# A two-layer decoder step: thirteen matmuls at the start, two key products placed earlier, and the fourth half's transpositions placed ahead of the next step's scores

## The chip, the cores and the metric

One NeuronCore of a Trainium2 chip runs the whole program. The metric is the device time of one execution in microseconds (us). TensorE is called PE here, VectorE DVE, ScalarE ACT, GpSimd POOL and SyncE SP; PEld is PE's weight load, which has rows of its own in the profile.

## The reference, cut to what matters

Two decoder layers are applied to 1024 prompt tokens and to 32 sample tokens (8 sequences of 4), which share the weights; the kernel holds them as one block of 1056 columns.

```python
def trunk_layer(x, ...):
    h = rmsnorm(x, nm_pre)
    q_abs, q_pe, c_kv, k_pe, u, v = project(h, pos, w_in, q_norm, w_uq, kv_norm, w_uk, v_norm)
    a_out = attend(q_abs, q_pe, c_kv, k_pe, w_uv)        # latent attention, 8 heads
    g_out = chunk_gating(u, v, w_s, b_s)                 # u * (tril(W_s) v + b), chunks of 128
    x = x + rmsnorm(concat(a_out, g_out) @ w_out, nm_post)
    f = square(relu(rmsnorm(x, nf_pre) @ w_up)) @ w_down
    x = x + rmsnorm(f, nf_post)
```

The prompt attends to its own 1024 keys, causally. Each sample sequence attends to 4096 cached keys besides its own four; they lie in pages of 128 keys that a page table names, so they are gathered page by page.

## The kernel before, in words

Each engine has one program of its own, written out by hand in order, and semaphores join them. Nothing is reordered by a scheduler: what stands ahead on an engine runs ahead. An fp32 product of PE shows as two records each of PE and PEld (two passes).

**Start.** PE waits for the first loads and multiplies the input by the first two column blocks of `w_in` in plain fp32 (L2432, 48 products, 96 records), with the mean of squares between (L2428). Beside it DVE adds up the squares, then makes the low parts `hl` of all eight input blocks (L1684), then takes PE's first accumulators (`take_z`, L1784). The third column block is the first product of split operands (L2479, `dense`). It writes the banks of the first block, so it waits on `acc_free`, which DVE's first `take_z` raises.

**From the projections to the attention.** A loop over nine token blocks (t = 0 to NB, NB = 8) transposes `v` (`turn_v`, L2595), makes one of eight units of q (`q_unit`, L2584) and mixes a chunk (`mix`, L2609). The last `mix` waits for DVE's `bias` of the chunk before (L1863), as both use PSUM bank 7. Behind the loop come eight small products for the sample queries (L2651), a wait for the last q unit, the keys of the first pair of heads (`keys_of`, L2629, two products of 512 columns), the values (`vals_of`, L2616), transpositions of the latent (`turn_c`, L2623 and L2624), the first scores (L2681), more keys and values, and then the steps. ACT and DVE copy each of these out of PSUM. SP first issues the loads of rotated queries and keys, then 16 DMAs of cache pages for step 0 (`gather(0)`, L541). Step 0 needs them at its first `turn_keys` (L2728), and PE waits there on `cache_in`.

**The steps.** Sixteen steps (c = 0 to 15) a layer interleave two things. The prompt's attention has 64 halves: a half i is one head of a job (pair of heads u, query block j), with j in the order 0, 7, 1, 6, 2, 5, 3, 4, and step c takes halves 4c to 4c+3. The paged attention takes 512 cached keys of four sequences a step. A half passes through `scores` on PE (L2681, with the mask in L2684), `maxima` on DVE (L1934), `exps` on ACT (L1189), `normalise` on DVE (L1940, L1943), `turn_p` on PE (L2693, up to 4 transpositions for n = 0 and the rest for n = 1), copies of these out of PSUM (`take_pt`: n = 0 by ACT L1204, n = 1 by DVE L1957), and `values` on PE (L2708, one call for both halves of a job), whose result ACT (L1198) and DVE (L1950) take. The transpositions share two PSUM banks in turn (the ring): each waits until what stands two places ahead has been copied out. The paged part of a step is `turn_keys` (L2728), `step_scores` (L2739, L2741), `step_max` on DVE (L2000), `step_exp` on ACT (L1226, behind `exps(i + 4)` there), `step_turn` (L2749) and `step_values` (L2758); the last two run in the next step. `WIDE_LAST` is true for every step, since the second job of each has j of 4 or more. `following(i)` is `scores(i)` with all its blocks. Each step begins with `values` of the second job of the step before:

```python
                for c in range(STEPS):
                    i, wide_last, first = 4 * c, WIDE_LAST[c], c % CHUNKS == 0
                    if c > 0:
                        values(2 * c - 1)
                        step_turn(c - 1)
```

Of the kernel before, what the change touches and what calls it, by code (L numbers as in the profile page):

```python
# [179 lines left out]
def build(nc, xT, wst, gains, pre, wuq, wuk, wuv, wsp, bsp, cache_c, cache_k, pages, consts,  # L180
          yT, o_cp, o_kp, o_cs, o_ks, o_vs, x_spill):
    with ExitStack() as ctx:
# [1466 lines left out]
        def _(dve):  # L1649
# [38 lines left out]
            for l in range(DEPTH):  # L1688
# [264 lines left out]
                def take_pt(i):  # L1953

                    n = JOBS[i // 2][1] - 3
                    turned(("p", i, 1))
                    dve.tensor_copy(pts[2 * (i % 2) + 1][:, 0:n, :],  # L1957
                                    ring_bank(("p", i, 1))[:, 0:n * P].rearrange(
                                        "p (k n) -> p k n", k=n)).then_inc(t_dve.sem, 1)
# [36 lines left out]
                def step_max(c):  # L1996

                    s = (c % CHUNKS + 1) % 2
                    dve.wait_ge(ds_full.sem, at.value(ds_full, c + c // CHUNKS + 2))
                    dve.tensor_reduce(stat[:, 22:23], ps[7][:, :], AX.X, ALU.max, negate=True)  # L2000
                    dve.drain()
                    dve.tensor_tensor(stat[:, 10 + s:11 + s], stat[:, 22:23], stat[:, 10 + 1 - s:11 + 1 - s],
                                      ALU.min).then_inc(dmax.sem, 1)
# [40 lines left out]
                for c in range(STEPS):  # L2044
                    i, wide_last, first, last = 4 * c, WIDE_LAST[c], c % CHUNKS == 0, c == STEPS - 1
                    if c > 0:
                        take_o(2 * c - 1)
                    if not wide_last:
                        take_pt(i)
                    normalise(i + 1)  # L2050
                    if c > 0:
                        take_ropes(c)
                    maxima(i + 2)
                    if first:
                        new_max(c // CHUNKS)
                    if wide_last:
                        take_keys(c, 2)
                        if c == 0:
                            dve.wait_ge(outs.sem, at.value(outs, 64))
                            take_ropes(c)  # L2060
                        normalise(i + 2)
                    else:
                        take_pt(i + 1)
                        normalise(i + 2)
                        take_keys(c, 2)
                    maxima(i + 3)

                    normalise(i + 3)
                    take_o(2 * c)
                    if c > 0:  # L2070
                        step_out(c - 1)
                    if wide_last:
                        take_pt(i + 2)
                        step_max(c)
                    if not last:
                        maxima(i + 4)
                    if wide_last:
                        take_pt(i + 3)
                    if first:
                        new_out(c // CHUNKS)  # L2080
                    if not wide_last:
                        step_max(c)
                    if not last:
                        normalise(i + 4)
                        maxima(i + 5)
                    if i + 3 in K_AT and K_AT[i + 3][1] == 1:
                        more_keys(K_AT[i + 3][0])
                    step_sum(c)
# [326 lines left out]
        @block.tensor  # L2415
        def _(pe):
            pe.wait_ge(s_init, 2)
            pe.wait_ge(nxt_new.sem, 2)
            for k, units in [(k, (0, 1)) for k in range(KD - 2)] + [(k, (u,)) for u in range(2) for k in (KD - 2, KD - 1)]:
                pe.wait_ge(s_x[k], 16)  # L2420
# [16 lines left out]
            for l in range(DEPTH):  # L2437
# [204 lines left out]
                for t in range(NB + 1):  # L2642
                    if t < NB:
                        turn_v(t + 1)
                    if 0 < t < UNITS_Q:
                        q_unit(t)
                    mix(t)

                pe.wait_ge(vt_free.sem, at.value(vt_free, NB + 1))
# [142 lines left out]
                                     k == first, k == last)  # L2792
                    return ins

                keys_of(0, 0, key_bank(0, 0)[:, :]).then_inc(k_full.sem, 1)
                keys_of(0, 1, key_bank(0, 1)[:, :]).then_inc(k_full.sem, 1)
                for kb in range(4):
                    vals_of(kb)
                pe.wait_ge(mix_free.sem, at.value(mix_free, NB + 1))
# [34 lines left out]
# [5 lines that stand above are left out]
                    for h in range(2):  # L2839
                        turn_p(i + h, 0)  # L2840
                        if h == 1 and not wide_last:
                            turn_p(i + h, 1)
                        scores(i + h + 2, 0)
                        if h == 0 and not wide_last:
                            turn_p(i + h, 1)
                        turn_keys(c, 2 * h)
                        if wide_last:
                            scores(i + h + 2, 1)
                        turn_keys(c, 2 * h + 1)
                        if first and h == 0:  # L2850
                            new_scores(c // CHUNKS)
                        if first and h == 1:
                            new_turn(c // CHUNKS)

                    values(2 * c)
                    if c > 0:
                        step_values(c - 1)
                    if first:
                        new_values(c // CHUNKS)
                    turn_p(i + 2, 0)  # L2860
                    if wide_last:
                        turn_p(i + 2, 1)
                        step_scores(c)
                    following(i + 4)
                    if not wide_last:
                        step_scores(c)
                    turn_p(i + 3, 0)
                    if wide_last:
                        turn_p(i + 3, 1)
                    following(i + 5)  # L2870
                    if i + 3 in K_AT:
                        u, h = K_AT[i + 3]
                        keys_of(u, h, ring(("k", u, h))).then_inc(t_full.sem, 1)
                    if c == STEPS - 1:
                        take_tile()
                        at.step(acc_free)
                        pe.wait_ge(acc_free.sem, at.value(acc_free, -2))
                        pe.wait_ge(exped.sem, at.value(exped, HALVES))
                        pe.wait_ge(gate_l.sem, at.value(gate_l, NB + 1))
                        out_part(0, (4, 5, 6, 7))  # L2880
                        step_turn(c)
                    if c == CHUNKS:
                        pe.wait_ge(on_new.sem, at.value(on_new, 1))
                        pe.transpose(ring(("f", 0))[:, 0:P], oacc[0], ident).then_inc(t_full.sem, 1)
# [374 lines left out]
```

## Time and profile before

| | |
|---|---|
| median of 3 runs | 2466.19 us (2462.88 to 2470.29) |
| the profiled execution | 2470.1 us, span 2468.3 us |
| mean granted PE clock | 0.996 |
| PE busy | 2423.9 us (98%) |
| DVE busy | 1547.9 us (63%) |
| ACT busy | 1021.5 us (41%) |

The time of an execution is a little longer than the span, which reaches from its first instruction to its last. A busy PE is not a PE at its peak, as its records overlap; what counts is the distance between the starts of records. A granted clock of 1.00 is 2.4 GHz and of 0.50 is 1.2 GHz.

### The profile page before, as it was taken

The numbers are of one execution on the slowest core, as the hardware profiler recorded it, in microseconds if no ns is written. First come the engines' busy times: TensorE is split into PE (matmuls) and PEld (weight loads), VectorE is DVE, ScalarE is ACT, GpSimd is POOL, SyncE is SP. The second block draws the span as 40 slices with busy tenths as digits, with TensorE's granted clock in tenths as the row PEclk, the third lists the DMA queues.
The fourth block names the chain that finished last, engine by engine and source line by source line (L and its number), as shares of the span: only waits on it lengthen the run. The fifth ranks groups of instructions, "written<-read, shape, count | busy, mean of one in ns | idle before, by whom it ended". The sixth has DMA issues, their size and how long they took to land.

```text
span 2468.3 us, 49447 instructions
## 1 busy us (share of the span) xinstructions
PE 2423.9 (98%) x19652; PEld 2196.8 (89%) x19652; DVE 1547.9 (63%) x1992; ACT 1021.5 (41%) x1536; POOL 926.8 (38%) x395
## 2 busy tenths in 40 slices
PE   8999999999999999999999999999999999999998
PEld 6996666898999999999979966669889999999998
DVE  5546676349776557755674566662597576557646
ACT  3224666327434333433441255662384333333334
POOL 2432000212664566455213410003046654665441
PEclk9999999999999999999999999999999999999999
DMA  6214333314636544563431143333237356545643
GB/s 218 64 39 112 97 92 85 123 62 147 221 146 219 208 161 150 211 218 138 157 120 46 39 125 92 91 86 114 96 113 296 107 184 225 193 139 181 217 146 152
DMA packets 182355, 347.55 MB, mean 141 GB/s; under 512 B 33968, under 2 KB 46448, under 8 KB 181424
## 3 DMA queue, kind: packets, MB, share of 16 engines
q1 hardware_dynamic: 116128, 207.12, 26.1%
q10 hardware_dynamic: 63504, 129.77, 14.5%
q0 software_dynamic: 2560, 8.39, 1.2%
q8 instruction: 114, 1.87, 0.3%
q14 instruction: 49, 0.40, 0.1%
HBM read 292.94 MB, written 49.06 MB: 139 GB/s over the span
## 4 chain that ended last, share of the span: by engine, by line
PE 89%; DVE 6%; ACT 2%; DVEq 1%; issue 1%; DMA 0%; ACTq 0%; SPq 0%
PE psum L2993 23%; PE psum L3040 21%; PE psum L2479 13%; PE psum L2681 5%; PE psum L2708 3%; PE psum L2464 3%; PE psum L2521 3%; PE psum L2693 3%; PE psum L2728 2%; PE psum L2584 2%; PE psum L2540 2%; PE psum L2432 1%; PE psum L2741 1%; PE psum L2739 1%; PE psum L2758 1%
## 5 line engine op out<-in xcount | busy, mean ns | idle before, releaser
L3040 PE MATMUL psum<-hidh,wh 128*128 128x264 f32 x1312 | 374.1, 285 | 9.6 <-DVE z L2194 5.3
L3040 PE MATMUL psum<-hidl,wh 128*128 128x264 f32 x1312 | 373.6, 285 | 0.0
L3040 PE MATMUL psum<-hidh,wl 128*128 128x264 f32 x1312 | 373.0, 284 | 0.0
L2993 PE MATMUL psum<-hh,wh 128*128 128x264 f32 x1280 | 363.4, 284 | 0.1
L2993 PE MATMUL psum<-hh,wl 128*128 128x264 f32 x1280 | 362.9, 283 | 0.0
L2993 PE MATMUL psum<-hl,wh 128*128 128x264 f32 x1280 | 362.6, 283 | 0.0
L2185 DVE TENSOR_TENSOR z<-psum,z 128x528 f32<-128x528 f32 x336 | 226.1, 701 | 88.2 <-PE psum L3040 88.2
L3040 PEld LDWEIGHTS psum<-hidh,wh 128*128 128x128 f32 x1312 | 246.6, 188 | 11.4 <-issue 8.2
L3040 PEld LDWEIGHTS psum<-hidh,wl 128*128 128x128 f32 x1312 | 247.3, 188 | 0.0
L3040 PEld LDWEIGHTS psum<-hidl,wh 128*128 128x128 f32 x1312 | 247.0, 188 | 0.0
L2993 PEld LDWEIGHTS psum<-hh,wh 128*128 128x128 f32 x1280 | 240.5, 188 | 0.5 <-issue 0.5
L2993 PEld LDWEIGHTS psum<-hh,wl 128*128 128x128 f32 x1280 | 240.6, 188 | 0.0
L2993 PEld LDWEIGHTS psum<-hl,wh 128*128 128x128 f32 x1280 | 240.5, 188 | 0.0
L2479 PE MATMUL psum<-hh,wh 128*128 128x352 f32 x720 | 233.2, 324 | 0.0
L2479 PE MATMUL psum<-hh,wl 128*128 128x352 f32 x720 | 231.1, 321 | 0.0
L2479 PE MATMUL psum<-hl,wh 128*128 128x352 f32 x720 | 230.9, 321 | 0.0
L803 POOL TENSOR_TENSOR wh<-raw,ones 128x1024 fp32r<-128x1024 f32 x36 | 73.4, 2038 | 341.3 <-PE psum L2479 252.2
L819 POOL TENSOR_TENSOR wl<-raw,wh 128x1024 fp32r<-128x1024 f32 x42 | 108.7, 2589 | 187.3 <-ACT wh L1381 184.7
L2175 DVE TENSOR_TENSOR hidl<-z,hidh 128x1056 fp32r<-128x1056 f32 (+1 forms) x100 | 163.6, 1636 | 9.8 <-ACT hidh L1367 9.8
L918 POOL DMA_INDIRECT z<-cache_k,krows x32 | 31.4, 980 | 357.9 <-DVE cn L1970 353.6
L819 POOL TENSOR_TENSOR wl<-sacc,wh 128x1024 fp32r<-128x1024 f32 x38 | 91.5, 2409 | 147.5 <-ACT wh L1381 129.8
L2479 PEld LDWEIGHTS psum<-hh,wh 128*128 128x128 f32 x720 | 135.1, 188 | 1.1 <-issue 0.3
(336 smaller groups left out, 5943.2 us busy)
## 6 DMA issues: line engine op xcount, KB each, us to landing
hh<-h_quarters ACTq DMA_DIRECT2D x60, 1056.0 KB, 5.5
hl<-h_quarters ACTq DMA_DIRECT2D x60, 1056.0 KB, 7.6
raw<-wst SPq DMA_DIRECT2D x48, 512.0 KB, 3.6
z<-cache_c SPq DMA_DIRECT2D x352, 64.0 KB
x<-x_spill SPq DMA_DIRECT2D x4, 4224.0 KB, 14.6
sacc<-wst SPq DMA_DIRECT2D x56, 256.0 KB, 3.2
t<-wst SPq DMA_DIRECT2D x56, 256.0 KB, 3.0
cn<-wst SPq DMA_DIRECT2D x56, 256.0 KB, 4.3
```

What stands on the lines that cost most here:

```text
L803: pool.tensor_tensor(wh[:, s, :], src, ones[:, 0:1].to_broadcast([P, TW]), ALU.mult)
L819: pool.tensor_tensor(wl[:, s, :], src, wh[:, s, :].bitcast(F32), ALU.subtract).then_inc(split.sem, 1)
L2175: dve.tensor_tensor(hid_of(t, hidl)[:, ks, :], src[:, ks, :], hid_of(t, hidh)[:, ks, :].bitcast(F32), ALU.subtract).then_inc(hid_l.sem, 1)
L2185: dve.tensor_tensor(part, dn_banks(u), part, ALU.add).then_inc(dn_free.sem, 1)
L2464: ins = pe.matmul(bank3(u, g), w, m[:, k, cols(g)], start=(first and n == 0), stop=(last and n == 2))
L2479: ins = pe.matmul(bank3(u, g), w[:, s, o:o + P], m[:, k, cols(g)], start=(k == 0 and n == 0), stop=(k == kk - 1 and n == 2))
L2521: ins = pe.matmul(bank, u_w[w], m[:, k, cols(g)], start=(first and n == 0), stop=(last and n == 2))
L2681: ins = pe.matmul(ps[2 * e + h][:, 0:w], qs[e][0:KQ, u, tok(j)], keys[0:KQ, 2 * (u % 2) + e, 512 * h:512 * h + w], start=True, stop=not last)
L2693: ins = pe.transpose(bank[:, (kb % 4) * P:(kb % 4 + 1) * P], probs[e][:, kb * P:(kb + 1) * P], ident)
L2708: ins = pe.matmul(prompt_o[v:v + 32, :], vals[:, kb, 2 * u * VD + v:2 * u * VD + v + 32], pts[2 * e + kb // 4][:, kb % 4, :], start=(kb == ...
L2993: ins = pe.matmul(psum[:, up_bank(st, u) + q, 0:HW], w[:, o:o + P], m[part], start=(fresh and k == 0 and n == 0), stop=(k == 3 and n == 2) ...
L3040: ins = pe.matmul(psum[:, 2 * u + q, 0:HW], w[:, o:o + P], m[:, t, k * HB + q * HW:k * HB + q * HW + HW], start=(fresh and k == 0 and n == ...
```

## The change

Three edits. PE runs 13 products of a 128x128 block of ones with itself, into PSUM bank 7, before it waits for its first load. The first two `keys_of` move from behind the loop over token blocks into its last round, ahead of `mix(8)`; there they wait for seven q units taken by DVE, not for eight. In each step `turn_p(i + 3)` moves ahead of `following(i + 4)` on PE, and on DVE `take_pt(i + 3)` moves ahead of `maxima(i + 4)`.

```diff
@@ vector
+                    if wide_last:
+                        take_pt(i + 3)
                     if not last:
                         maxima(i + 4)
-                    if wide_last:
-                        take_pt(i + 3)
                     if first:
                         new_out(c // CHUNKS)
@@ tensor
             pe.wait_ge(s_init, 2)
+            pe.wait_ge(s_init, 2)
+            for _ in range(13):
+                pe.matmul(ps[7][:, 0:P], ones[:, :], ones[:, :], start=True, stop=True)
             pe.wait_ge(nxt_new.sem, 2)
@@
                     if 0 < t < UNITS_Q:
                         q_unit(t)
+                    if t == NB:
+                        pe.wait_ge(q_dve.sem, at.value(q_dve, UNITS_Q - 1))
+                        keys_of(0, 0, key_bank(0, 0)[:, :]).then_inc(k_full.sem, 1)
+                        keys_of(0, 1, key_bank(0, 1)[:, :]).then_inc(k_full.sem, 1)
                     mix(t)
@@
-                keys_of(0, 0, key_bank(0, 0)[:, :]).then_inc(k_full.sem, 1)
-                keys_of(0, 1, key_bank(0, 1)[:, :]).then_inc(k_full.sem, 1)
                 for kb in range(4):
                     vals_of(kb)
@@
+                    turn_p(i + 3, 0)
+                    if wide_last:
+                        turn_p(i + 3, 1)
                     following(i + 4)
                     if not wide_last:
                         step_scores(c)
-                    turn_p(i + 3, 0)
-                    if wide_last:
-                        turn_p(i + 3, 1)
                     following(i + 5)
```

PE at the end of the loop over token blocks in layer 0, from the mixing of chunk 7 (64x128) on, before. The 64x32 row is `mix(8)`, L2651 the sample queries, and L2629 the keys:

```order
L2609 MATMUL psum<-scratch 64x128 x8
L2609 MATMUL psum<-scratch 64x32 x8
L2651 MATMUL psum<-free_a,cn 128x32
L2651 MATMUL psum<-free_b,cn 128x32
...
L2629 MATMUL psum<-z,sacc 128x512 x2
L2616 MATMUL psum<-rinv,z 128x512 x4
```

The same place in the changed kernel, where `mix` is L2612, the keys L2632, the sample queries L2658 and the values L2619:

```order
L2612 MATMUL psum<-scratch 64x128 x8
L2632 MATMUL psum<-z,sacc 128x512 x2
L2612 MATMUL psum<-scratch 64x32 x8
L2658 MATMUL psum<-free_a,cn 128x32
L2658 MATMUL psum<-free_b,cn 128x32
...
L2619 MATMUL psum<-rinv,z 128x512 x4
```

The two key products moved past `mix(8)` and the eight small products.

PE in step 6 of layer 0, from `step_scores(6)` (L2739, L2741) to `values` of its second job (L2708), before:

```order
L2739 MATMUL psum<-z,sacc 32x512 x4
L2741 MATMUL psum<-cn,sacc 128x512
L2681 MATMUL psum<-scratch,free_a 128x512
L2684 MATMUL psum<-trir,idr 128x128
L2693 MATMUL psum<-cst,z 128x128 x6
L2681 MATMUL psum<-scratch,free_b 128x512
L2684 MATMUL psum<-trir,idr 128x128
L2708 MATMUL psum<-t,scratch 32x128 x24
```

The same place in the changed kernel, where L2746 and L2748 are `step_scores`, L2700 is `turn_p`, L2688 and L2691 are `scores`, and L2715 is `values`:

```order
L2746 MATMUL psum<-z,sacc 32x512 x4
L2748 MATMUL psum<-cn,sacc 128x512
L2700 MATMUL psum<-cst,z 128x128 x6
L2688 MATMUL psum<-scratch,free_a 128x512
L2691 MATMUL psum<-trir,idr 128x128
L2688 MATMUL psum<-scratch,free_b 128x512
L2691 MATMUL psum<-trir,idr 128x128
L2715 MATMUL psum<-t,scratch 32x128 x24
```

The six transpositions moved ahead of the first of the two score blocks, so that both score blocks now stand between them and `values`.

DVE in step 0 of layer 0, from `step_max` (L2000, L2002) on, as a difference; L1957 is `take_pt(3)` and L1934 is `maxima(4)`:

```order
 L2000 TENSOR_REDUCE stat<-psum 128x1
 L2002 TENSOR_TENSOR stat<-stat 128x1
-L1934 TENSOR_REDUCE stat<-psum 128x1
-L1957 COPY t<-psum 128x512
+L1957 COPY t<-psum 128x512
+L1934 TENSOR_REDUCE stat<-psum 128x1
 L1991 COPY stat<-stat 128x1
 L1993 COPY z<-psum 128x128
```

The copy and the reduction have changed places. The orders of ACT, POOL and SP are the same in both kernels.

## Rows read from the trace of the kernel before

**Rows 1.** Page: the chain that ended last, by engine

```profile
PE 89%; DVE 6%; ACT 2%; DVEq 1%; issue 1%; DMA 0%; ACTq 0%; SPq 0%
```

**Rows 2.** Windows: stretch, length, busy by engine, granted clock, DMA share, GB/s

```profile
201.50:208.30 6.80, 6.80 (x18) 4.15 (x18) 4.65 (x14) 3.29 (x6) 2.36 (x3) 0.50 0.53 117
1423.50:1430.30 6.80, 6.80 (x15) 3.80 (x15) 4.35 (x14) 2.98 (x6) 2.76 (x3) 0.50 0.58 129
608.50:611.00 2.50, 0.95 (x8) 0.76 (x8) 2.41 (x3) 1.19 (x3) 0.00 (x0) 1.00 0.67 210
```

**Rows 3.** Timeline of the start, PE and PEld: start, us, instruction, count

```profile
7.98 20.85 PE L2432 MATMUL psum<-x,z 128*128 128x352 f32 x60 [7.98 <-DMA x<-xT]
...
13.39 0.34 PEld L2432 LDWEIGHTS psum<-x,z 128*128 128x128 f32 x1 [0.25 <-issue]
...
13.88 14.39 PEld L2432 LDWEIGHTS psum<-x,z 128*128 128x128 f32 x49
...
41.12 0.19 PEld L2479 LDWEIGHTS psum<-hh,wh 128*128 128x128 f32 x1
```

**Rows 4.** Timeline of the start, DVE

```profile
23.59 15.53 DVE L1684 SCALAR_TENSOR_TENSOR hl<-x,gpre,hh 128x1056 fp32r<-128x1056 f32 x8
...
39.11 1.25 DVE L1784 TENSOR_TENSOR z<-psum,rinv 128x1056 f32<-128x1056 f32 x1
```

**Rows 5.** Timeline of PE ahead of the steps, layer 0

```profile
198.24 1.09 PE L2609 MATMUL psum<-scratch 128*64 128x128 f32 x16
200.22 0.65 PE L2609 MATMUL psum<-scratch 32*64 32x32 f32 x16 [0.89 <-DVE scratch L1863]
...
203.74 3.78 PE L2629 MATMUL psum<-z,sacc 128*128 128x512 f32 x4
...
222.00 0.60 PE L2728 MATMUL psum<-cst,z 128*128 128x128 f32 x4
```

**Rows 6.** DMA ahead of the steps: SP's queue, then windows of both layers

```profile
208.00 10.05 SPq L541 DMA_DIRECT2D z<-cache_c  x16
...
219.20:222.00 2.80, 2.74 (x11) 1.23 (x10) 1.71 (x6) 1.82 (x6) 0.00 (x0) 1.00 0.00 0
1440.00:1443.60 3.60, 3.60 (x13) 1.61 (x12) 2.61 (x7) 2.72 (x10) 0.00 (x0) 1.00 0.00 0
```

**Rows 7.** Timeline of PE, layer 1: its first `turn_keys`

```profile
1443.64 0.60 PE L2728 MATMUL psum<-cst,z 128*128 128x128 f32 x4
```

**Rows 8.** Lines of PE in the steps of layer 0: busy, mean ns, idle before, releasers

```profile
L2708 PE MATMUL psum<-t,scratch 128*32 128x128 f32 x1152 | 38.1, 275 | 4.2 <-ACT t L1204 1.8 <-DVE z L1993 1.0 <-DVE t L1957 0.9
```

**Rows 9.** Timeline of PE and ACT, end of step 3, layer 0

```profile
276.84 0.60 ACT L1204 ACTIVATE t<-psum 128x512 f32<-128x512 f32 x1 [2.31 <-PE psum L2693]
...
277.78 1.30 PE L2708 MATMUL psum<-t,scratch 128*32 128x128 f32 x40 [0.58 <-ACT t L1204]
```

**Rows 10.** Timeline of PE, end of step 12, layer 0

```profile
406.51 0.60 PE L2681 MATMUL psum<-scratch,free_a 96*128 96x256 f32 x2
...
409.45 1.96 PE L2708 MATMUL psum<-t,scratch 128*32 128x128 f32 x64 [0.91 <-DVE t L1957]
```

**Rows 11.** Timeline of DVE, end of step 12, layer 0

```profile
406.63 0.69 DVE L1957 COPY t<-psum 128x512 f32<-128x512 f32 x1
...
408.07 0.42 DVE L1934 TENSOR_REDUCE stat<-psum 128x1 f32<-128x256 f32 x1
408.41 0.68 DVE L1957 COPY t<-psum 128x512 f32<-128x512 f32 x1
```

**Rows 12.** Timeline of PE, DVE and ACT, end of step 6, layer 0

```profile
320.37 0.82 PE L2693 MATMUL psum<-cst,z 128*128 128x128 f32 x6
...
320.57 0.69 DVE L1934 TENSOR_REDUCE stat<-psum 128x1 f32<-128x512 f32 x1
...
322.17 0.69 ACT L1226 ACTIVATE z<-psum,stat 128x512 f32<-128x512 f32 x1
...
323.56 0.66 PE L2749 MATMUL psum<-cst,z 128*128 128x128 f32 x4
```

## The prediction

> **What bounds the kernel now.** I read the page first. PE sets the end: 89% of the chain that ended last is PE, 6% DVE [rows 1]. So an edit pays only where PE starts something earlier that it does not then wait for. Next I asked the windows for the granted clock, since a span can be full of PE records and still be slow: it is 1.00 nearly everywhere, but 0.50 from 201.5 to 208.3 us in layer 0 and from 1423.5 to 1430.3 in layer 1 [rows 2]. Those are the stretches between the projections and the attention. The first matmuls are slow too, which the clock column does not tell (no clock record lies ahead of them). The loads do: at 13.39 one takes 0.34 us behind 0.25 idle, 0.59 a record, and from 13.88 on 49 take 14.39 us, 0.294 a record [rows 3]. So PE began at 1.2 GHz at 7.98 and came to 2.4 GHz near 13.8 us. Last I read the timelines around the three edits, to see who would hold PE if PE were earlier, and the groups by line inside the steps, where `values` (L2708) has 4.2 us of idle time ahead of it per layer [rows 8]; the same stretch of layer 1 gives the same row.
>
> **Edit 1, the thirteen products at the start.** They are 26 records of 128 columns. The nearest fp32 row, 6 transpositions of 128 columns in 0.82 us [rows 12], is about 0.14 a record, so 0.28 at the lower clock: 7.3 us at most. PE now waits until 7.98 for its input [rows 3], so they lie in that wait, save for some tenths if PE is slow to start them. If the clock has risen by 7.98, the 60 records up to L2428 take 60 x 0.294 = 17.6 us instead of 20.7, and PE is 3.1 us earlier. Who holds it then? The first split product (L2479, loads at 41.12 [rows 3]) writes banks that DVE's L1784 must free, and that ends at 39.11 + 1.25 = 40.36. Ahead of it DVE has the eight L1684, 15.53 us from 23.59 without a gap to L1784 [rows 4]: DVE never waits for PE there, so it will not move. PE can start at about 40.36 + 0.13 = 40.5, not at 38.0. The gain is 41.12 - 40.5 = **0.6 us**, and PE gets a new pause of about 2.4 us.
>
> The Trainium skill (TensorE: Matmul & The Clock Gate, Part 1) says that the throttled state is the default and activity releases it, and its Terms put the penalty at the throttled time times (1 - K/N). By that the warm-up would be worth half of the 5.8 us of slow records, 2.9 us, and the sum below 12.4 instead of 10.1. The rows agree on the two levels, but not on what this is worth here, as DVE sets the date.
>
> **Edit 2, the keys.** Before, mixing chunk 7 is over near 199.3, PE is idle 0.89 us until 200.22 (it waits for DVE's L1863), and the keys start at 203.74, at the lower clock: 4 records in 3.78 us [rows 5], about half of that at 2.4 GHz. Afterwards they run from 199.3 to 201.0. `mix(8)` starts 0.8 us later than now. Behind it DVE does not suffer: its L1863 for that block comes long after. So 1.7 us of work goes into a pause of 0.9 plus a delay of 0.8 that is earned back where the keys stood: 0.9 us gained. The second part is the clock. It fell at 201.5, 1.3 us behind that pause and the small products on both sides of it. With 1.7 us of dense work in the pause I take it to stay at 1.00. A stretch with only 0.95 us of PE in 2.50 kept 1.00 elsewhere [rows 2]. The work of 6.8 us then takes 3.4: 3.4 us gained. PE would come to the first `turn_keys` 4.3 us earlier, at 222.00 - 4.3 = 217.7 in layer 0 and 1443.64 - 4.3 = 1439.3 in layer 1 [rows 5, 7].
>
> There stands what is late next: the gather of step 0. SP issues its 16 DMAs from 208.00 for 10.05 us, behind loads whose dates DVE and POOL set, and none of that moves. DMA is busy until about 219.2 and silent from there on, in layer 1 until 1440.0 [rows 6]. So PE goes on at about 219.35 and 1440.1: 222.00 - 219.35 = **2.65 us** in layer 0, 1443.64 - 1440.1 = **3.5 us** in layer 1. Everything behind is issued in order from there. Of the 8.6 us that PE gains, 2.4 are lost to the gather.
>
> **Edit 3, the steps.** PE is nearly gapless in them; idle time stands ahead of `values` alone, 4.2 us a layer [rows 8]. It waits there for the copies of the transpositions, which now have only one score block as cover; with two, the copies come earlier. That bounds the gain at 8.4 us. But DVE holds it. Step 12: DVE ends `step_max` at 408.07, does `maxima` (0.34 to the next start), then the copy at 408.41, and `values` starts 1.04 later at 409.45 [rows 10, 11]. With the two exchanged, the copy starts at 408.07, if its transpositions are there. They would start at 406.51, but the last four wait for the bank that DVE empties by 407.3, and are done near 408.0. `values` then starts at 409.11: 0.34 gained of 0.91. Step 0 has the same widths and gives about the same. In step 3 the last copy is behind ACT's 276.84 + 0.60 [rows 9]. Afterwards DVE's copy, behind `step_max` at 277.0, ends at about 277.3 and `values` starts near 277.6: 0.15 of 0.58; steps 7 and 11 are alike. Steps 1 and 13 I put at 0.25 each. With 512 columns in the score block (step 6) there is no idle time to win. Per layer 2 x 0.35 + 3 x 0.15 + 2 x 0.25 = 1.65, **3.3 us** for both, and the ends are 0 and 8.4; I take the lower part, since I can name DVE's date in each.
>
> What is pushed back: the first score block, by up to 0.65 us in step 6. `maxima` follows at about 321.2 instead of 320.57, and ACT's two exponentials follow it. `step_turn` at 323.56 waits for L1226, now over at 322.9 [rows 12]: 0.7 of slack for 0.5 of delay. That cover costs nothing, but it is thin.
>
> **Sum.** 0.6 + 2.65 + 3.5 + 3.3 = 10.1 us. The profiled execution, 2470.1 (span 2468.3 and 1.8 around it), becomes 2460.0. It was 3.9 above the median of the runs, so against 2466.19 the sum gives **2456.1 us**.
>
> **The rivals.**
> - *The clock falls in a pause that the change makes.* PE gets pauses of 2.4 us ahead of L2479 and of 1.6 and 0.7 us ahead of `turn_keys`; before 201.5 it fell at a pause of 0.89 with light work beside. For: the new pause at the start is longer than the 1.55 us in the window at 608.5, which is the longest that kept 1.00. Against: dense products stand on both sides. One fall as long as the old ones costs up to 3.4 us of PE (6.8 x 0.5), half that if it is half as long; the sum is then 7 to 8 and the time about 2459. If the old fall also stays in both layers, only about 2 x 0.9 is left of edit 2, the sum is near 6 and the time 2460. The skill's same page (Part 1, HAM oscillation and the psum-queue failure mode) holds that short idle times between groups throw the clock back; by that this rival would be the rule. In the steps it is not borne out: 0.9 us pauses at their ends left the clock at 1.00. I give it 27%.
> - *The start pays in full*, because DVE's L1684 are short if POOL's work beside them falls otherwise. Then 3.1 instead of 0.6: 2453.6. DVE's rows have no gap to close, so 4%.
> - *The new order holds PE in the steps.* The score block comes 0.65 us later, DVE puts 0.34 to 0.6 of copy ahead of `maxima`, and the chain `maxima`, `exps`, `step_exp`, `step_turn` has 0.7 of slack. If both delays add (0.65 + 0.42 = 1.07), each of some 30 steps loses 0.35, 10.5 us, and the 3.3 are gone as well: sum -3.7, about 2470. Against it: DVE does the copy in the time in which it would wait for the later scores. It decides from 1.0 us of delay on, as 0.3 a step uses up the other gains. 5%.
> - *The gain ahead of the steps is lost further on*, for instance as loads for rotated keys or the copies of ACT and DVE hold PE before `turn_keys`: edit 2 gives 2 us, the sum 6, 2460. 9%.
> - My forecast: 55%.
>
> **How the numbers follow.** A measurement of this kernel can tell about 0.3% (7.4 us) from no change. The forecast and the full start lie beyond that bound, with scatter (the runs before spread over 7.4 us) most of their 59% but not all; of the first and fourth rival about half does. That gives 0.72 faster, 0.23 the same and 0.05 slower. The range goes down by the part of 8.4 and of 3.1 that I left out, to 2449, and up to the sum of 4 or so of the weaker cases, 2463.
>
> **What the profile after would show.** Edit 1: loads of 0.19 from 7.98 on; L1784 still near 39.1; the first split product near 40.5 behind DVE. Edit 2: keys from about 199 less 0.6; a granted clock of 1.00 up to the steps; PE idle ahead of the first `turn_keys`, released by DMA. Edit 3: L2708's idle time down from 4.2 to about 2.5 a layer, and none new ahead of L2749 or L2693. The prediction is wrong if the clock column shows 0.50 again, if L1684 moved, if the gather moved, or if L2749 has waits.

## The result, and the profile after

The changed kernel takes 2469.99 us (median of 22 runs, 2467.43 to 2471.47), the kernel before 2466.60 (22 runs, 2462.59 to 2471.53). The ratio is 1.0013, with a 95% interval of 1.0007 to 1.0019. So the change costs about 3 us: less than the 0.3% that the prediction called measurable in one comparison, and outside its range of 2449 to 2463.

The page and the granted clock of the changed kernel first. The chain answers to [rows 1]: PE went from 89% to 84% of it, so more of the chain is something that PE waits for.

```profile
span 2468.8 us, 49500 instructions
...
PE 84%; DVE 8%; ACT 2%; issue 2%; DVEq 2%; DMA 1%; SPq 0%; ACTq 0%; POOL 0%; POOLq 0%
```

Then the windows of the changed kernel (stretch, length, PE busy with its records, granted clock, DMA share, GB/s), beside [rows 2]:

```profile
41.00:44.40 3.40, 3.40 (x14) 0.50 0.45 171
...
204.80:208.20 3.40, 3.40 (x5) 0.51 0.77 175
...
1426.90:1430.20 3.30, 3.30 (x5) 0.50 0.91 200
```

Ahead of the last microseconds of the program the clock falls three times instead of twice. The old falls start 3.4 us later, end at the same dates as before and so last half as long, and a new one stands at 41.0 us. What is ahead of that one shows in the timeline of the start (start, length, instruction, count, idle time ahead of it), beside [rows 3, 4]:

```profile
1.14 5.88 PE L2420 MATMUL psum<-ones 128*128 128x128 f32 x26 [1.14 <-POOL eps L790]
7.49 1.42 PE L2435 MATMUL psum<-x,z 128*128 128x352 f32 x4 [0.47 <-DMA x<-xT]
...
38.97 2.41 DVE L1784 TENSOR_TENSOR z<-psum,rinv 128x1056 f32<-128x1056 f32 x2
...
40.47 0.40 PE L2482 MATMUL psum<-hh,wh 128*128 128x352 f32 x1 [2.25 <-DVE z L1784]
40.71 0.32 PE L2482 MATMUL psum<-hl,wh 128*128 128x352 f32 x1
...
41.33 0.49 PE L2482 MATMUL psum<-hl,wh 128*128 128x352 f32 x1
```

The thirteen products lie in the wait for the input and the first split product starts at 40.47, as predicted. But PE has stood still for 2.25 us ahead of it, and half a microsecond later its records take 0.49 us instead of 0.32.

The timeline of PE ahead of the steps answers to [rows 5, 7]:

```profile
200.17 1.98 PE L2632 MATMUL psum<-z,sacc 128*128 128x512 f32 x4
202.08 0.65 PE L2612 MATMUL psum<-scratch 32*64 32x32 f32 x16
...
220.46 0.60 PE L2735 MATMUL psum<-cst,z 128*128 128x128 f32 x4
...
1441.57 0.60 PE L2735 MATMUL psum<-cst,z 128*128 128x128 f32 x4
```

The keys take 1.98 us instead of 3.78 and the pause is gone. PE reaches the first `turn_keys` 1.54 us earlier in layer 0 (220.46 against 222.00) and 2.07 earlier in layer 1 (1441.57 against 1443.64).

In the steps this lead is lost. From the first `turn_keys` to the last `values` (the one at 457.26 us in the kernel before, 457.49 in this one) PE takes 235.26 us in the kernel before and 237.03 in the changed one: 1.8 us more in layer 0, and 1.8 in layer 1 in the same way. The waits of PE in the steps of layer 0 say where (line, what it waited for: us in all, times, longest). First the kernel before, then the changed one (its L2715 is L2708 of before, L2735 is L2728 and L2700 is L2693):

```profile
PE psum L2708 <- ACT t L1204: 1.8, 3, 0.6
PE psum L2708 <- DVE z L1993: 1.0, 1, 1.0
PE psum L2708 <- DVE t L1957: 0.9, 1, 0.9
```

```profile
PE psum L2715 <- DVE t L1957: 1.2, 3, 0.5
PE psum L2735 <- ACT cn L1233: 0.9, 4, 0.2
PE psum L2700 <- DVE t L1957: 0.8, 3, 0.3
PE psum L2715 <- DVE z L1993: 0.4, 1, 0.4
...
PE psum L2700 <- DVE z L1943: 0.3, 1, 0.3
```

The idle time ahead of `values` did shrink, from 4.2 [rows 8] to 1.7 us, even below the 2.5 that was forecast. Two waits are new and come several times: `turn_keys` for ACT's copy L1233 (`step_pt`), and the transpositions L2700 (`turn_p`) for DVE's copy L1957. The third new one, for `normalise` (L1943), comes once, in step 0. Here are the first two in the timeline of the changed kernel: the end of step 2 on PE and ACT, and step 12 on PE.

```profile
264.75 1.02 PE L2688 MATMUL psum<-scratch,free_a 96*128 96x512 f32 x2
265.99 0.63 PE L2735 MATMUL psum<-cst,z 128*128 128x128 f32 x4 [0.21 <-ACT cn L1233]
...
264.41 0.69 ACT L1189 ACTIVATE z<-psum,stat 128x512 f32<-128x512 f32 x1 [0.54 <-DVE stat L1934]
...
265.25 0.60 ACT L1233 ACTIVATE cn<-psum 128x512 f32<-128x512 f32 x1
...
406.93 0.60 PE L2700 MATMUL psum<-cst,z 128*128 128x128 f32 x4
407.80 0.65 PE L2700 MATMUL psum<-cst,z 128*128 128x128 f32 x4 [0.26 <-DVE t L1957]
```

And the end of step 2 in the kernel before, PE and ACT:

```profile
266.51 1.02 PE L2681 MATMUL psum<-scratch,free_a 96*128 96x512 f32 x2
267.37 0.60 PE L2728 MATMUL psum<-cst,z 128*128 128x128 f32 x4
...
265.76 0.69 ACT L1189 ACTIVATE z<-psum,stat 128x512 f32<-128x512 f32 x1 [0.55 <-DVE stat L1934]
...
266.60 0.60 ACT L1233 ACTIVATE cn<-psum 128x512 f32<-128x512 f32 x1
```

`turn_keys` writes the bank of the ring that `step_pt` empties. Before, `turn_keys` starts 0.86 us behind the score block (267.37 - 266.51) and `step_pt` had started 0.77 us ahead of it. Afterwards it starts 1.24 behind it (265.99 - 264.75) and right at the end of `step_pt`: PE loses 0.38 us. ACT's `step_pt` is 0.41 us later against PE's score block than it was. It stands behind an exponential (L1189) that waits for a `maxima`, and this one stands on DVE behind the `normalise` of the half before, which needs that half's exponential, its `maxima` and its score block. That score block is the one that now comes behind the transpositions. In step 12 PE starts transposition 5 of the fourth half 0.87 us behind the first (407.80 - 406.93), where four take 0.44: 0.43 lost. It needs the bank that DVE's copy of the third half frees, and the score block that used to cover that copy has been moved away.

### The profile page after: what moved, and what is told of

The parts are those of the page before. It is cut to its first block, busy times and chain, and to the rows that moved or that the text cites. A ratio compares the mean times of both kernels' runs of the same rounds, so it can differ in the third digit from the quotient of the medians.

```text
span 2468.8 us, 49500 instructions
## 1 busy us (share of the span) xinstructions
PE 2430.2 (98%) x19678; PEld 2198.4 (89%) x19678; DVE 1547.3 (63%) x1992; ACT 1021.7 (41%) x1536; POOL 928.8 (38%) x395
## 4 chain that ended last, share of the span: by engine, by line
PE 84%; DVE 8%; ACT 2%; issue 2%; DVEq 2%; DMA 1%; SPq 0%; ACTq 0%; POOL 0%; POOLq 0%
PE psum L2998 22%; PE psum L3045 21%; PE psum L2482 13%; PE psum L2688 4%; PE psum L2467 3%; PE psum L2524 3%; PE psum L2715 2%; PE psum L2735 2%; PE psum L2700 2%; PE psum L2587 2%; PE psum L2543 2%; PE psum L2748 1%; PE psum L2746 1%; PE psum L2765 1%; PE psum L2554 1%
```

## The experiments

All times are beside runs of the kernel before on the same chip: 11 runs of each kernel, and 33 of the kernel before for the first eight rows, 27 for the last three. Where the text gives the length of a stretch or the date of a product, it is from the one profiled execution of each kernel.

| kernel | median us | ratio to before | 95% interval |
|---|---|---|---|
| edit 1 alone | 2467.85 | 1.0002 | 0.9993 to 1.0011 |
| edit 2 alone | 2465.80 | 0.9995 | 0.9986 to 1.0004 |
| edit 3 alone | 2469.97 | 1.0012 | 1.0003 to 1.0021 |
| the kernel before again | 2465.75 | 0.9996 | 0.9987 to 1.0005 |
| edit 3, ACT's order mended | 2467.02 | 1.0000 | 0.9991 to 1.0009 |
| edit 3, first four transpositions only | 2470.05 | 1.0012 | 1.0003 to 1.0021 |
| edit 3 in six steps only | 2464.06 | 0.9985 | 0.9976 to 0.9994 |
| edit 1, its pause filled | 2466.30 | 0.9999 | 0.9990 to 1.0008 |
| edit 2, six steps | 2462.69 | 0.9988 | 0.9979 to 0.9997 |
| the same, and the filled edit 1 | 2462.56 | 0.9984 | 0.9975 to 0.9993 |
| all three, ACT's order mended | 2465.58 | 0.9997 | 0.9988 to 1.0006 |

### The three edits apart, and the kernel before again

Each of the first three is the kernel before with one edit of the diff.

Edit 1 alone:

> Edit 1 alone (the 13 products at the start). My theory after the trace of the changed kernel: the products raise the clock early, but DVE's L1784 holds TensorE for about 2.3 us near 40.5 us and the clock falls to 0.50 right behind that pause, which costs more than the 0.6 us that DVE's date leaves: 0.5 to 1.5 us slower than before, with a 0.50 stretch starting at 41 us. Rival (the prediction's term): 0.6 us faster, no fall at 41.

The windows of that kernel show the fall, 3.4 us long:

```profile
41.90:45.30 3.40, 3.40 (x13) 0.50 0.64 222
```

From 66 us on its dense products start 0.83 us later than in the kernel before. Ahead of the fall PE stood still for 1.96 us. By the trace the theory holds; the timed difference of 0.5 us is inside the interval.

Edit 2 alone:

> Edit 2 alone (keys ahead of the last mixing chunk). My theory: it gives about 2.4 us in each layer, since the clock still falls between the projections and the steps but for a shorter time, so 4 to 5 us faster than before. Rival 1 (the prediction's terms): 2.65 and 3.5, 6.2 us faster, with the clock at 1.00 up to the steps. Rival 2: what is gained ahead of the steps is lost in them as ACT or DVE hold TensorE there: under 2 us faster.

Its profiled execution has a granted clock of 1.00 from 13.4 us to the last stretch of the program. That makes it the test of the prediction's own case. Windows and waits of PE:

```profile
201.50:208.30 6.80, 6.80 (x32) 1.00 0.59 130
...
13.40:2460.00 2446.60, 2411.86 (x19643) 1.00 0.41 140
```

```profile
PE psum L2732 <- DMA z<-cache_c: 1.9, 1, 1.9
```

PE reaches the first `turn_keys` (L2732 here) with 1.9 us to spare and waits for the gather, as the prediction said (it had 4.3 - 2.65 = 1.65). In layer 1 the same wait is 1.2 us (it had 0.8). `turn_keys` starts at 219.52 and 1439.2 us, 2.5 and 4.4 us earlier than before. Of this PE had 0.4 us of lead already at 190 us, ahead of the edit, and 1.7 at 1403 us, so the edit gave 2.1 us in layer 0 and 2.7 in layer 1, where 2.65 and 3.5 were forecast. The gather did not stay where it was: in layer 1 SP issues it from 1428.3 us against 1429.6 before, 1.3 us earlier where PE was 1.7 ahead. Behind it SP issues stores (from L629 on) at 1437.8 us, before the gather has landed; in the kernel before they came at 1443.3, long after it. Whether they slow it down no run shows. Even against the profiled execution of before with its two falls the gain is 4.3 us (spans of 2464.0 and 2468.3), not 6.2. The timed runs gain less still, 0.7 us by the medians and 1.6 by the means (the interval includes no change), and neither expectation, 4 to 5 or 6.2, came true. Rival 2 named the right size, but not the reason: nothing is lost in the steps, where the lead stays at 2.5 us to the end of the layer. The reason that I find lies in the kernel before, next.

The kernel before again:

> The kernel before once more, unchanged, as a second profile of it. My theory: its profiled execution of 2470.1 us lay 3.5 above its median because the clock's falls at 201.5 and 1423.5 lasted 6.8 us each in it; another execution has falls at other times or shorter ones and ends up to 3 us earlier. Rival: the falls are the same in every execution, and a profiled execution is always some 3 to 4 us above the median. The ratio to before is 1.000 in both.

Its profiled execution had the same two falls of 6.8 us again (at 201.9 and 1423.9), and took 2469.43. So the trace did not show the other case. The granted clock that comes with each timed execution did:

| mean granted clock | before: executions, mean us | changed kernel | edit 2 alone |
|---|---|---|---|
| 0.996 and 0.997 | 42, 2468.3 | 7, 2470.6 | none |
| 0.998 | 17, 2466.2 | 12, 2469.6 | 7, 2465.7 |
| 0.999 and 1.000 | 34, 2464.9 | 3, 2468.4 | 4, 2464.8 |

(The 93 executions of before are those that stood beside the experiments.) By their clock a third of them have hardly any fall; they take 2464.9, and the 42 with the lowest clock take 3.3 us more. At the ends, five at 0.996 take 2469.8 and three at 1.000 take 2463.7, 6 us apart. The trace of the kernel with ACT's order mended (below), which has no fall ahead of the steps though its order there is that of before, gives the same size: against the kernel before with its two falls it gets 2.7 us ahead at the first place and 3.2 at the second. Both theories were partly wrong: the length of the falls varies, but they lasted 6.8 us in both profiled executions of before; and a profiled execution is not always above the median, as that kernel's was the fastest of its 11.

Does edit 2 shorten the falls? Eight profiled executions lack it, with 16 such places in two layers: the fall lasted 6.8 us in eight, 3.4 in six and did not come in two. Five have it, with 10 places: it never lasted 6.8 us, lasted 3.4 in five and did not come in five. That speaks for it. The timed runs don't decide it: edit 2 alone has no execution at 0.997 or below, but neither have the 33 of edit 3 alone, of its first four transpositions and of its six steps, which lack edit 2. At a high clock edit 2 gives nothing (2464.8 against 2464.9, only four executions of it). That fits the trace without falls: there PE, without edit 2, waits 0.6 us for the gather in layer 0 and in layer 1 comes 0.4 us behind the gather's last packet, so an earlier PE would gain next to nothing.

Edit 3 alone:

> Edit 3 alone (the fourth half's transpositions ahead of the next step's score blocks). My theory: it costs about 1.8 us in each layer, by a new hold of TensorE of 0.3 to 0.4 us at turn_keys(c, 0) where ACT's step_pt is late: 3 to 4 us slower than before. Rival (the prediction's term): 3.3 us faster. Second rival: the loss in the changed kernel's steps comes from their earlier start behind edit 2, and edit 3 alone is within 1 us of before.

Its waits are those of the changed kernel. From the first `turn_keys` to the last `values` PE takes 1.67 us more than before in layer 0 and 1.76 in layer 1. The theory holds in size: this edit is about the whole of the loss. In place it holds for the most part. From one first `turn_keys` of a step to the next, PE loses 0.34 to 0.42 us in steps 2, 6, 10 and 14 (1.5 us in layer 0), 0.46 in steps 4 and 8, where the last transpositions are held, and 0.25 in steps 5 and 9; in steps 1, 3, 7, 11, 12 and 13 it gains 1.3 in all.

### What costs in the steps

ACT's order, with edit 3:

```
                     if c > 0:
-                        if wide_last:
-                            exps(i + 1)
                         take_o(2 * c - 1)
                         step_pt(c - 1)
+                        if wide_last:
+                            exps(i + 1)
```

> Edit 3 alone, and ACT does take_o and step_pt ahead of exps(i+1). In the run of edit 3 alone TensorE loses 0.37 us at turn_keys(c+1, 0) behind steps 2, 6, 10 and 14 and 0.17 behind steps 5 and 9, held by ACT's step_pt, which stands behind an exponential that comes 0.4 us later than before. Theory: these holds vanish, 1.8 us a layer, and the holds of 0.43 us at the last transpositions in steps 4, 8 and 12 stay; edit 3 then costs 0 to 0.3 us a layer instead of 1.7. Rival: the whole chain of ACT and DVE is late by the 0.65 us of the score block, so TensorE is held at another place as much, and the cost stays at 1.7 us a layer (3.4 us slower than before).

The end of step 2 in its timeline, PE and ACT:

```profile
262.81 1.02 PE L2681 MATMUL psum<-scratch,free_a 96*128 96x512 f32 x2
263.68 0.60 PE L2728 MATMUL psum<-cst,z 128*128 128x128 f32 x4
...
262.58 0.60 ACT L1233 ACTIVATE cn<-psum 128x512 f32<-128x512 f32 x1 [0.28 <-PE psum L2749]
263.07 0.68 ACT L1189 ACTIVATE z<-psum,stat 128x512 f32<-128x512 f32 x1
```

`step_pt` now waits for PE and not PE for it, and `turn_keys` is back at 0.87 behind the score block. The stretch of the steps is 0.11 and 0.27 us longer than before instead of 1.67 and 1.76, and the time is that of before. The theory holds in size; the rival would have been 3.4 us slower. So ACT's place for `step_pt` carried 1.5 us of each layer's loss, that of steps 2, 6, 10 and 14. The holds behind steps 5 and 9 did not vanish: these steps still take 0.26 us more each. In step 5 0.15 of it lies ahead of the transpositions behind `step_turn`, not at `turn_keys`, so the expectation had them at the wrong place; what holds PE there stays open.

Only the first four transpositions moved:

```
                     turn_p(i + 3, 0)
-                    if wide_last:
-                        turn_p(i + 3, 1)
                     following(i + 4)
                     if not wide_last:
                         step_scores(c)
+                    if wide_last:
+                        turn_p(i + 3, 1)
```

> Of edit 3 only the first four transpositions of the fourth half come ahead of the score block, the others stay behind it, and DVE's order is as before. Theory: the hold of 0.43 us in steps 4, 8 and 12 comes from the ring of two banks (the transpositions 5 to 8 need the bank that DVE's copy of the third half frees), so it vanishes, as the score block covers the copy again; the gain at the value products vanishes too; what is left is the later score block, 0.44 us instead of 0.65, with holds at turn_keys of 0.1 to 0.2: 0 to 0.8 us a layer slower, 0 to 1.6 in all. Rival: the hold in steps 4, 8 and 12 is DVE being slow after its exchanged order, and the score block's place alone sets the rest: cost as in edit 3, 3.4 us.

Its waits of PE in the steps of layer 0:

```profile
PE psum L2708 <- DVE t L1957: 3.6, 6, 0.9
PE psum L2708 <- issue: 1.2, 4, 0.4
```

The mechanism was right and the size wrong. The wait of the transpositions for DVE's L1957 is gone, in all steps, so it did come from the ring of two banks: the score block covers that copy again. But the kernel is as slow as edit 3 (1.83 and 1.73 us more per layer, where 0 to 0.8 was expected): `values` now waits in steps 2, 6, 10 and 14 too, which it never did before. With the score block of 512 columns ahead of the last transpositions and DVE's `maxima` ahead of their copy, as in the old order, that copy is late by the four transpositions that stand ahead of the block. In the change the DVE exchange seems to avoid this wait; no run has the one without the other, so that is argued. These four steps lose 0.28 to 0.38 us each, 1.4 of the 1.83 in layer 0. So moving the score block back by even 0.44 us costs, at one place or another.

The steps in which edit 3 gained, alone. On PE, and in the same way for `take_pt(i + 3)` and `maxima(i + 4)` on DVE:

```
+                    early = c in (1, 3, 7, 11, 12, 13)
+                    if early:
+                        turn_p(i + 3, 0)
+                        turn_p(i + 3, 1)
                     following(i + 4)
...
+                    if not early:
                         turn_p(i + 3, 0)
                         if wide_last:
                             turn_p(i + 3, 1)
```

> Edit 3 in steps 1, 3, 7, 11, 12 and 13 alone, where the run of edit 3 showed TensorE gaining 0.24, 0.19, 0.16, 0.20, 0.32 and 0.24 us. Theory: the holds are local, each step with its own balance, so these six give 1.35 us a layer and none of the losses: 2.5 to 2.8 us faster than before. Rival: the gains were only the losses of the step ahead given back, and alone they give 0 to 0.5 us in all.

The waits in the steps are local: each step keeps its own balance, and the steps left alone take what they took before, within 0.07 us. The stretch of the steps is 1.30 us shorter than before in layer 0 and 1.39 in layer 1, and the kernel is 3.0 us faster by the medians, with an interval that lies wholly below a ratio of 1. The rival, 0 to 0.5 us, is out.

All three edits with ACT's order mended:

> The changed kernel with all three edits, and ACT does take_o and step_pt ahead of exps(i+1). Theory: the holds at turn_keys(c+1, 0) go here too, 1.6 us a layer, so it is 3.2 us faster than the changed kernel and within 0.5 us of before (2466 to 2467.5 us). Rival: in the changed kernel the steps start earlier or later than with edit 3 alone, other engines hold TensorE, and it stays 2 to 3 us slower than before.

The steps take 0.04 and 0.28 us more than before, the time is that of before. So the loss of the changed kernel as a whole is undone by the same exchange on ACT; what edits 1 and 2 do beside it adds up to nothing that these runs can tell.

### The start

Edit 1 with its pause filled, behind the products on the input, ahead of the wait for the first weights:

```
+            pe.wait_ge(mean_read.sem, NG)
+            for _ in range(10):
+                pe.matmul(ps[7][:, 0:P], ones[:, :], ones[:, :], start=True, stop=True)
             pe.wait_ge(s_first, 144)
```

> Edit 1, and ten more products of ones (20 records, 2.3 us at 2.4 GHz) in the pause that edit 1 makes ahead of the first split product. Theory: the clock fell at 41 us because TensorE stood 2.3 us idle ahead of it; with the pause filled it stays at 1.00, and edit 1 gives its 0.6 us (0.3 to 0.9) instead of costing 0.8 to 0.9 up to the attention of layer 0. Rival: the fall at 41 us has another cause (the weight loads or the kind of products ahead of it), it stays, and the filled version costs as much as edit 1 alone.

Timeline of PE and the window behind it:

```profile
38.53 2.39 PE L2441 MATMUL psum<-ones 128*128 128x128 f32 x20
40.68 0.40 PE L2485 MATMUL psum<-hh,wh 128*128 128x352 f32 x1
...
41.40 0.32 PE L2485 MATMUL psum<-hl,wh 128*128 128x352 f32 x1
```

```profile
41.00:44.40 3.40, 3.40 (x23) 1.00 0.64 206
```

The clock stays at 1.00, and from 66 us on PE is 0.65 us ahead of the kernel before instead of 0.83 behind it. The pause was the cause of the fall: it came in all three kernels with the pause (2.25, 1.96 and 1.96 us of idle) and in neither of the two with it filled. But the length of a pause does not tell by itself. In this kernel PE is idle for 2.32 us between the products of ones and its first input, and the clock, which rose at 4.0 us, stays at 1.00; edit 2 alone has a pause of 1.92 us without a fall. Filled against not filled, the fall is worth 1.5 us at 66 us. The 0.65 us, in contrast, is the distance to a single trace of before, and is not shown to be a gain: seven other executions with the old start came to this place between 0.1 us later and 1.4 us earlier than that trace, as their input came and their clock rose at other dates. No timed gain can be told (ratio 0.9999).

The Trainium skill (TensorE: Matmul & The Clock Gate, Part 1, the psum-queue failure mode) tells of a kernel in which TensorE idles for short times between groups of matmuls, so often that its clock swings between the two levels. The traces agree in that short idle times can bring the clock down; here it was a single one of 2.25 us, with the fall behind it, and none when it is filled.

### Together

Edit 2 with the six steps:

> Edit 2, and edit 3 in steps 1, 3, 7, 11, 12 and 13 alone; no edit 1. Theory: the parts add. Edit 2 alone had a mean 1.4 us below before, since it lets TensorE reach the gather of step 0 also where the clock falls; the six steps gave 2.7 to 3.0. So 4 to 4.5 us faster than before, and its runs lie within 3 to 4 us of each other where those of before spread over 7 to 9. Rival: they share the same slack (ACT and DVE at the start of the steps) and together give 3 us at most.

3.0 us faster by the ratio where 4 to 4.5 was expected: that is the rival's figure, and by the intervals (2.2 us to either side) it can't be told from the theory's. The profiled execution shows something that neither had. Timeline of PE at the first `turn_keys` of layer 1 (L2735 here), and the window around it:

```profile
1437.50 1.11 PE L2735 MATMUL psum<-cst,z 128*128 128x128 f32 x4 [1.23 <-DMA z<-cache_c]
```

```profile
1437.30:1440.60 3.30, 3.10 (x9) 0.50 0.76 186
```

By the end of the wait for the gather, which edit 2 makes, the clock has fallen. The steps take 1.47 us less than before in layer 0, but 0.31 more in layer 1, where the six steps alone had taken 1.39 less. So the fall took 1.7 us back. In the trace of edit 2 alone the same two waits (1.9 and 1.2 us) had no fall behind them; how often it comes no run tells.

The runs are closer together, as expected: 2461.22 to 2464.72 against 2463.65 to 2470.52 of before.

The same with the filled edit 1:

> As the kernel with edit 2 and the six steps, and the warm-up with its pause filled (13 products ahead of the input, 10 more ahead of the first split product). Theory: that adds its 0.4 to 0.7 us, as DVE's L1784 sets the date behind it: 4.5 to 5.2 us faster than before. Rival: the earlier start makes no difference, since the gather of step 0 holds TensorE anyway: as the kernel without it, 4 to 4.5.

3.9 us faster than before by the ratio (3.4 by the medians), less than the 4.5 to 5.2 expected and too close to the kernel without the filled start to separate them. Of all versions it has the lowest median, 2462.56, and its interval of 0.9975 to 0.9993 lies below no change: it beats the kernel before, and with it the changed kernel, which is slower than that one.

## Why the prediction was wrong, point by point

The sum was 10.1 us of gain; what came is a loss of 3.4 by the medians. The parts run alone, as means of their runs against the mean of before beside them (2466.96): edit 1 +0.5, edit 2 -1.6, edit 3 +2.9, together +1.8. The changed kernel has +3.0 in the same way. The intervals (2.2 us to either side for each part) allow this difference.

**Edit 3, the step that failed most: "0.7 of slack for 0.5 of delay. That cover costs nothing, but it is thin."** It was 3.3 us of gain in the sum and measured 3.4 of loss, 1.67 and 1.76 a layer. The gain itself was sized well: 1.30 and 1.39 in the six steps, for which 1.30 was forecast; step 0, with another 0.35, gave nothing, as its transpositions wait for DVE themselves. The slack was read at one waiter, `step_turn` (L2749), and there it held: in step 2 it went from 0.63 us (265.58 against the end of L1226 at 264.95) to 0.22, and there is no wait. But the same delayed chain goes on to `maxima(i + 5)`, `exps(i + 5)`, `take_o` and `step_pt`, and the instruction that waits for its end is `turn_keys`, through the ring of banks. There the slack was almost none: in the kernel before `turn_keys` starts 0.17 us behind the end of `step_pt`, and 0.14 behind it where it is held. This place carried 1.5 us of a layer's loss; steps 4 and 8 carried 0.9 and steps 5 and 9 0.5, against the 1.3 gained. The rival "the new order holds PE in the steps" had the right kind of mechanism and the right sign at the wrong place, and 5% was too little for it. That its time, about 2470, is the measured one is luck: it rested on 10.5 us of loss by holds at `step_turn` in 30 steps, of which there was none, and on the full gains of the other edits.

**The ring, a step seen and not priced: "the last four wait for the bank that DVE empties by 407.3".** The text used this only to date the copy. It is also a stop of PE, 0.43 us in steps 4, 8 and 12 (0.87 us between two groups of four transpositions instead of 0.44), and in steps 4 and 8 there was no idle time ahead of `values` to pay it with. In step 12 the forecast of 0.34 gained came out as 0.32 all the same, since there the stop is taken from 0.91 us of idle.

**Edit 2, the term 2.65 + 3.5.** The mechanism was right and the size too large. With the clock at 1.00 PE waits 1.9 and 1.2 us for the gather, against 1.65 and 0.8 forecast, and gains 2.1 and 2.7 us. The sentence "none of that moves" left out that the gather of layer 1 moves with the lead, but not by all of it. What failed in part is "I take it to stay at 1.00": in the changed kernel's trace the falls are still there, at half their length, and the lead is 2.45 and 2.40 us over the edit (0.91 late to 1.54 early, and 0.33 late to 2.07 early). Not all of that need be the edit's doing, as in the traces of edit 3 alone, without edit 2, the falls last 3.4 us too. And what failed for the timed result is the last line of the sum, "It was 3.9 above the median of the runs, so against 2466.19 the sum gives 2456.1". Those 3.9 us were, as it seems, the clock's falls themselves. A third of the executions of before don't have them. The same microseconds were counted once as a gain of edit 2 and once as the distance to the median. This is inferred from the granted clocks of the runs; both profiled executions of before have the falls.

**Edit 1, the term 0.6.** The date was right, 40.47 against 40.5, and so was the pause of 2.4 us (2.25). The rival "the clock falls in a pause that the change makes" came true at this place: a fall of 3.4 us cost 1.5, by the traces with the pause filled and not filled, and turned the gain into 0.8 to 0.9 of loss. The 0.6 itself was the distance to one trace. Executions with the old start began the first split product between 40.05 and 41.35 us (three of them between 40.6 and 40.85, where edit 1 alone has 40.7), so how much of it an average execution has to give is not shown.

**The range**, 2449 to 2463, reached up only as far as weaker gains. Its only case in which an edit loses in the steps had 5% and lay outside it.

## What to carry to other kernels

When an edit delays work that another engine needs, follow the delay to the end of its chain and look at every buffer that the chain's last copy frees, not only at the first waiter: here the ring bank of `turn_keys` was three operations behind the one that was checked. A block that stands between two users of a small ring is cover, even where nothing is idle; move it only in steps whose idle time pays for it. And before pricing what a profile shows of the clock, see whether the other runs have it too: an execution above the median may owe its distance to the very thing that the edit removes.

## What was not expected of the hardware

- The falls of the clock ahead of the steps are not a property of the program alone. The same kernel has executions with 0.996 and with 1.000, 2469.8 and 2463.7 us on average. In the eight traces without a warm-up the first rise came between 9.7 and 14.2 us, with PE's first product between 6.5 and 8.3, and each fall ahead of the steps lasted 3.4 or 6.8 us or did not come. Pauses of 1.9 and 2.3 us had no fall at their end or behind them, and pauses of 1.2, 2.0 and 2.25 us had one.
- The idle time that the trace reports understates a stop of PE. In step 12 it is 0.26 us, while the next record starts 0.43 late; at `turn_keys` 0.21 for 0.38. The reported waits of PE in the steps of layer 0 fell from 4.6 to 4.0 us in the change, and the stretch still grew by 1.8 us. The start times of the same instruction in two traces, not the sums of idle time, gave the balance.
- The 26 records of 128 columns at the lower clock took 5.88 us, 0.226 each, less than the 0.28 that was estimated from transpositions.
